# In the expert stage, DVE writes hid one weight split earlier, its low part one split earlier, and the overflow list step stands between them

## The reference, cut to what matters

```python
for e in range(N_EXPERTS):
    y = (jax.nn.silu(t @ w_g[e]) * (t @ w_u[e])) @ w_d[e]
    out = out + gate[:, e:e + 1] * y.astype(jnp.float32)
```

## Time and profile before

| | us |
|---|---|
| median of 3 runs | 710.39 (707.74 to 710.98) |
| span of the profiled execution | 706.8 |
| PE busy | 682.5 (97%) |
| DVE busy | 522.9 (74%) |
| ACT busy | 425.1 (60%) |
| POOL busy | 142.2 (20%) |
| DMA, mean rate over the span | 240 GB/s |
| subtractions of L1477 for wl, 96 | 218.5 busy, 2.29 each |
| high parts of L935 for wh, 96 | 182.3 busy, 1.92 each |

### The profile page before, as it was taken

How to read it: one execution, slowest core, us unless ns; L and a number is a source line. 1 busy time by engine, 2 the same in 40 slices (tenths; PEclk the granted TensorE clock), 3 DMA queues, 4 the chain that set the end, 5 groups by cost and what they waited for, 6 DMA issues and landing times.

```text
span 706.8 us, 9503 instructions
## 1 busy us (share of the span) xinstructions
PE 682.5 (97%) x3514; PEld 546.5 (77%) x3514; DVE 522.9 (74%) x686; ACT 425.1 (60%) x607; POOL 142.2 (20%) x160
## 2 busy tenths in 40 slices
PE   8999999999899999999999999999999999999992
PEld 5899788777666777788888778888888888888871
DVE  5347655565887674766557998899999999988884
ACT  6746734244664443554333478888888888888881
POOL 4202850021001010100001202222222222222135
PEclk9999999999999999999999999999999999999997
DMA  8733232403772000230094699999999999999864
GB/s 298 248 97 155 95 141 83 168 0 135 282 297 77 1 1 1 86 123 1 33 355 163 236 420 393 387 379 371 388 369 375 375 375 380 375 378 386 323 211 165
DMA packets 33155, 161.23 MB, mean 228 GB/s; under 512 B 6221, under 2 KB 6555, under 8 KB 18396
## 3 DMA queue, kind: packets, MB, share of 16 engines
q1 hardware_dynamic: 23680, 140.40, 51.2%
q0 software_dynamic: 5344, 10.27, 5.4%
q10 hardware_dynamic: 4092, 10.07, 4.0%
HBM read 149.59 MB, written 20.03 MB: 240 GB/s over the span
## 4 chain that ended last, share of the span: by engine, by line
PE 73%; DVE 14%; DMA 5%; ACT 3%; issue 2%; POOL 1%; SPq 0%; POOLq 0%; ACTq 0%; DVEq 0%
PE pj L2204 38%; PE scores L2204 18%; PE tr_v L2204 10%; DVE wl L1477 4%; PE tr_a L2212 2%; PE scores L2673 2%; DMA fin<-acc_rows 2%; DVE w_lo L1506 2%; DMA acc_rows<-y,idx_sb 1%; PE tr_v L2212 1%; PE tr_a L2702 1%; DVE hid L1477 1%; DMA raw<-in_dense 1%; POOL rs L777 1%; ACT w_hi L977 1%
## 5 line engine op out<-in xcount | busy, mean ns | idle before, releaser
L1477 DVE TENSOR_TENSOR wl<-moe_raw,wh 128x2048 fp32r<-128x2048 f32 x96 | 218.5, 2290 | 23.8 <-ACT wh L935 23.0
L935 ACT ACTIVATE wh<-moe_raw 128x2048 fp32r<-128x2048 f32 x96 | 182.3, 1920 | 32.5 <-PE scores L2204 12.0
L775 POOL TENSOR_SCALAR rs<-stat 128x1 f32<-128x1 f32 (+4 forms) x31 | 14.0, 451 | 303.7 <-DVE stat L1698 152.2
L2204 PE MATMUL pj<-w_hi,xT_hi 128*128 128x512 f32 (+2 forms) x176 | 64.4, 367 | 0.8 <-ACT w_hi L977 0.6
L829 POOL DMA_INDIRECT acc_rows<-y,idx_sb x14 | 22.3, 1590 | 205.5 <-ACT y L1399 191.5
L2204 PE MATMUL pj<-w_hi,xT_lo 128*128 128x512 f32 (+2 forms) x176 | 62.3, 354 | 0.0
L2204 PE MATMUL pj<-w_lo,xT_hi 128*128 128x512 f32 (+2 forms) x176 | 60.9, 352 | 0.0
L2204 PE MATMUL pj<-wh,xgh 128*128 128x512 f32 x128 | 51.5, 403 | 0.2 <-issue 0.2
L2204 PE MATMUL tr_v<-wh,xgh 128*128 128x512 f32 x128 | 51.2, 400 | 0.0
L1506 DVE SCALAR_TENSOR_TENSOR w_lo<-raw,pack_a,w_hi 128x512 fp32r<-128x512 f32 (+2 forms) x64 | 44.0, 745 | 9.3 <-ACT w_hi L977 9.2
L2204 PE MATMUL scores<-wh,hTh 128*128 128x512 f32 x128 | 49.9, 390 | 0.6 <-DVE hTl L1477 0.6
(11 more groups left out here) (458 smaller groups left out, 1522.6 us busy)
## 6 DMA issues: line engine op xcount, KB each, us to landing
moe_raw<-in_w_exp_gate SPq DMA_DIRECT2D x32, 1024.0 KB, 10.7
moe_raw<-in_w_exp_up SPq DMA_DIRECT2D x32, 1024.0 KB, 11.7
moe_raw<-in_w_exp_down SPq DMA_DIRECT2D x32, 1024.0 KB, 12.3
raw<-in_dense SPq DMA_DIRECT2D x16, 1024.0 KB, 6.7
raw<-in_dense SPq DMA_DIRECT2D x8, 256.0 KB, 6.0
x_rows<-in_x_prompt SPq DMA_DIRECT2D x4, 512.0 KB, 10.6
xw<-in_x_prompt ACTq DMA_DIRECT2D x1, 2048.0 KB, 8.5
h_rows<-h ACTq DMA_DIRECT2D x4, 512.0 KB, 4.0
```

The source lines that it names most:

```text
L775: link(pool.tensor_scalar(rs[rows, n, cs], stat[rows, n, cs], EPS, None, ALU.add))
L935: act.activation(wh[s4][:, :], moe_raw[n % RING][:, :], ACT.Copy).then_inc(hi_done, 1)
L1477: return dve.tensor_tensor(out, a, b, op)
L2204: return pe.matmul(out, lhsT, rhs, start=start, stop=stop, skip_group_check=True)
```

## The change

In steps 0 to 14 DVE's order is changed; no instruction is added or removed, and no other engine's order is changed.

```diff
                 for j in range(3, 9):
+                    if j == 4:
+                        hidden(e, 6 * e + 4)
                     if j == 5:
-                        hidden(e, 6 * e + 4)
-                    if j == 6:
+                        if 2 <= e <= 10:
+                            extra_lists(e - 2)
                         hid_lo(e, b)
                     if e == E - 2 and j == 6:
                         dve.wait_ge(last_tok_T, 1)
                         dve.tensor_scalar(shared[:, :], px[0][:, 0:P], next_tok, None, ALU.is_equal).then_inc(shared_ready, 1)
                     split_lo(e, b, j)
-                if 2 <= e <= 10:
-                    extra_lists(e - 2)
```

## The result

The changed kernel takes 712.3 us (median, 710.88 to 714.65), beside 709.23 us (707.74 to 711.27) for the kernel before on the same chip; the ratio is 1.0037 [1.0019, 1.0055]. It is slower by 0.37%, some 2.6 to 3.1 us, where 709.8 us and a range of 706.5 to 711.6 had been forecast. The profiled execution of after took 712.79 us with a span of 710.8 us, 4.0 us more than the span of before.

What follows compares the result with a forecast made beforehand. PE was taken to bound the expert steps, with the DMA engines also at their limit; of 15 x 0.23 = 3.45 us the DMA-paced end would leave 0.6 us, so 710.4 - 0.6 = 709.8 us, range 706.5 to 711.6.

Steps and rivals of the forecast that it cites:

- What bounds the step: Expert steps: PE loses 0.23 us at each turn of hid; moving hid ahead shortens the step from 17.97 to 17.74 us.
- Low part, list step, the late slot: DVE's expert steps: low part and list step moves cost nothing; split 5's slot, freed 1.8 us later, costs nothing either.
- The DMA takes the gain: End of expert stage: of 3.45 us, at most 1.2 us survives, as the last weight loads land no sooner.
- The tail: Behind the expert stage: the end hangs on fin's landing; gain between 0 and 1.2 us, middle 0.6 us taken.
- fin: Load of the accumulated rows in the tail, landed at 687.33 before; forecast to land near 687 again.
- (b): Rival: the tail's row gathers share slow DMA engines with the last weight loads, costing up to 2.1 us: 712.5 us; chance 0.10.
- (c): Rival: the row gather becomes PE's bound in expert steps, step stays 17.97, 710.4 us; chance 0.10, shared with no effect.
- (a): Rival: landings move up with the issues, so the whole 3.45 us gain arrives: 706.9 us; chance 0.20.

Runs made afterwards that it cites:

- lighter loads: Each weight load of experts 2 to 15 cut to three of four column blocks: kernel before 708.58 us (0.9995), changed kernel 704.30 us (0.9944).
- the swap: ACT's last step writes hid's high part ahead of tile 2's square: on the changed kernel 710.06 us (0.9991), on the kernel before 709.23 us (0.9981).
- the late gather: The changed kernel with POOL's second row gather of the tail held back until tile 2 has landed: 710.59 us, ratio 1.0013.

## Why the prediction was wrong, and where it was right

**What bounds the step: right, with one part missing.** The turn of hid came 0.24 us after the matmul ahead (forecast 0.23) and the step was 17.72 us (17.74). But the 0.23 us was put down to hid alone, and the low part's move was costed at nothing, as covered by 1.2 us (457.3 less 456.1). The run with hid alone shows that without it the whole gain is lost again at the down half. The cover was taken from when the low part would end in the new order; where it would end with hid early and the low part in its old place wasn't asked.

**Low part, list step, the late slot: right.** hid waits 0.17 us (0.2); the wait for the high part is 0.85 us at most in steps without a list step, and 0 to 0.5 us are left of it in the steps with one; taking the list step back changes nothing. The late slot of split 5 costs no time that can be told.

**The DMA takes the gain: right, and sooner than said.** The lighter loads gave 704.3 us, so the traffic is the reason. ACT began to wait at the end of step 10 (601.97), not in the last two or three steps, and the last three distances of turns are the long ones. The estimate that the transfers of a step need 18.7 us came out: the last two distances are 19.07 and 18.58, 18.8 in the mean. The last weights landed at 675.71 and 678.23, against 675.1 and 677.6 in before; they didn't move up with the issues, as said. PE's last turn of hid gained 1.05 us, where 1.2 us at most had been allowed.

**The tail: this is the step that failed.** The prediction said: "A PE that is done sooner changes nothing unless fin lands sooner", and gave the gain at the end bounds of 0 and 1.2 us. The sentence by itself fits: with the swap PE ended 0.8 us sooner, tile 3 landed no sooner, and the time was before's. It isn't the whole, since fin alone changes nothing either: with fin 5.7 to 8.0 us sooner before's time stayed (the lighter loads). Two paths arrive together, as the prediction had read the earlier trace rows. What failed is the lower bound, the 0 for a landing of fin that "stands still". It held only if the landings did not move, and if nothing in the last step but the end waited for them. Neither holds: tiles 1 and 2 landed later, and hid's high part stands behind tile 2's square in ACT's queue. In before the square, read-out included, had ended at about 685.2 and PE's turn released the high part at about 685.9, a cover of 0.7 us. In after tile 2 landed 2.7 us later, which went through that cover, made PE wait 4.11 us and cost it the clock: +3.56 and +2.32 us against -1.05, where the prediction had -0.6 for all of it. The prediction read ACT's rows of the last step at the two weights and not on to its squares; fin's landing was treated as something that only the end of the kernel waits for.

**The tiles' landing.** "fin lands near 687 as before" held for tile 3, which the chain named (687.97, before 687.33). Tiles 1 and 2, which ACT's queue waits for, landed 2.6 and 2.7 us later, at 682.93 and 686.75. One landing time for four loads was the wrong resolution.

**The rivals.** (b), slower through the tail's gathers, had the region right, and the gather may have a share. But its carrier was to be the last weight, landing behind 679.18; this landed at 678.23, and the gathers issued only 0.5 us sooner than in before. Its price, 2.1 us, was for another wait than the one that came, so that its 712.5 us lies beside the measured 712.3 is luck. (c) shows up in the last three steps only, with 2.0 us of waiting for gathered rows on PE, and not by its own cause: the gathers took no longer, they went out later, behind ACT's waits for weights. (a) is what happens with lighter loads.

## What to carry to other kernels

A stage whose loads take longer from issue to landing with every step lives on its lead, even when its busiest engine still sets the step (before's step stayed 17.97 us with lighter loads). A faster engine spends that lead sooner and then waits for the transfers, and what this does at the end of the stage decides the sign. So before shortening such a stage, go through every in-order queue of its last step and note what waits for a load and what stands behind it; critical work whose data is there belongs ahead of work that waits for a landing. And where a chain has two halves, here hid and its low part, work out where the second one ends when only the first is moved.

## What was not expected of the hardware

**The price of a wait on PE.** After idling 4.11, 3.70 and 3.49 us PE came back at a granted clock of 0.50, with 512-column matmuls 0.43 us apart; the first of these stretches lasted 4.9 us, and the last down took 8.06, 8.20 and 8.55 us in place of 5.74. After 1.53 us it kept 1.00. After 2.78 us, in the run with the late gather, PE came back at 1.00 and fell only 1.4 us later, as the mean of 4 us and two stretches in it show:

```profile
689.00:693.00 4.00, 4.00 (x13) 3.10 (x13) 2.93 (x3) 2.38 (x5) 3.66 (x5) 0.65 0.54 194
688.80:690.00 1.20, 1.19 (x5) 1.01 (x6) 0.85 (x1) 1.11 (x3) 1.11 (x2) 1.00 0.47 106
690.40:693.20 2.80, 2.80 (x8) 2.21 (x7) 1.88 (x3) 1.15 (x2) 2.55 (x4) 0.50 0.54 212
```

That down took 7.35 us. So in this kernel a wait of 2.8 us cost 1.6 us beyond itself, and waits of 3.5 to 4.1 us cost 2.3 to 2.8, the shortest of them the most. The Trainium skill (TensorE: Matmul & The Clock Gate, Part 1: The HAM clock gate) has the same two levels and the fall after idling, and says that no others occur; the rows agree, with 1.00 and 0.50 in stretches that don't straddle a change.

**Landings keep their own pace.** In the eleven executions with full loads the last weight lands 277.1 to 278.9 us after the first turn of the stage where PE's steps are 17.97 us long, and 277.7 to 280.0 where they are 17.72. With PE ahead, the loads are issued sooner and land no sooner.
